# One queue instead of two for the cached pages of stick-breaking attention

## The chip, the cores and the metric

The kernel runs as one launch on one core of a Trainium2 chip. The metric is the device time of that launch in microseconds (us), lower is better. All arrays start in the device's memory (HBM) and the results go back there; the host only lays arrays out.

## The reference

One inference step of a two-layer decoder, for a prompt of 256 tokens and 8 sample sequences of 8 new tokens each. Every layer is a half-step SwiGLU, a token mixer and a second half-step SwiGLU; the weights are shared by all tokens. The first layer's mixer has two groups of heads: linear attention, and stick-breaking attention, to which the change belongs. Cut to that:

```python
def sb_mixer(q, k, v, q_base):            # per head, dh = 64, 8 heads
    z = einsum('bqhd,bkhd->bhqk', q, k) * dh ** -0.5
    before = k_pos[None, :] < q_pos[:, None]
    log_keep = where(before, log_sigmoid(-z), 0)
    after = cumsum(log_keep, axis=3, reverse=True) - log_keep
    w = where(before, exp(log_sigmoid(z) + after), 0)
    return einsum('bhqk,bkhd->bqhd', w, v)
```

For a sample sequence, k and v are 1024 cached rows followed by its 8 new ones. The cached rows lie in a pool of pages of 128 rows; a page table gives the 8 pages of each sequence. All data are 32-bit floats, so the keys of one page (128 rows by 8 heads by 64) are 256 KB, and so are its values.

## The kernel before, in words

The program is a row of stages, each a block in which every engine has its own instruction list and the lists meet only at semaphores; at the end of a block all engines wait for one another. The stages are: modulation, a feed-forward stage, the first layer's mixer (`even_stage`, from line 862), two feed-forward stages, the second layer's mixer, a last feed-forward stage. Feed-forward and projection weights stream through a ring of four 2 MB slots.

Inside the first mixer, `stick_prompt` (line 908) computes stick-breaking attention of the prompt, and `stick_sample` (line 1071) that of the 8 samples, two sequences at a time: STEPS is 4, and step g handles sequences 2g (called s = 0 in the code) and 2g + 1 (s = 1). There is one buffer of keys for each s (`K[0]`, `K[1]`, 2 MB each, eight pages) and one of values (`VV[0]`, `VV[1]`), so nothing is double-buffered across steps: the keys of step g can be loaded only when the logits of step g - 1 are done, and its values when the outputs of step g - 1 are done.

One step on TensorE (list from line 1137): wait for all 16 key pages of both sequences (line 1144) and for the queries; 32 products queries by cached keys (line 1149) and 16 by the new keys (line 1153), then `logit_ready`; wait for the weights, which ScalarE and VectorE work out (lines 1199 to 1203 and 1223 to 1232); turn them by 9 transposes (lines 1161, 1164); wait for all value pages of both sequences (line 1166); 144 products weights by values (line 1174), then `out_ready`; two transposes of the result (line 1179), which VectorE copies out (line 1248).

Loads are made by `load_pages` (line 894). For each of 8 pages it reads the page number from the table into a register with a bounds check (line 899), waits once, before the first page, for a semaphore if one is given (line 901), and issues one DMA of 256 KB (line 905). Before the change each sequence of a pair has an issuing engine of its own, by the helper `loads_of` (line 1105): SyncE (queue SP) for s = 0 and GpSimd (queue POOL) for s = 1. Each of the two does, in this order: the values of step 0 with the new rows (line 1110, 16 KB); then, for g from 1 to 3, the keys of g after `logit_ready` of g - 1, the values of g after `out_ready` of g - 1, and the new rows. The keys of step 0 are loaded in `stick_prompt`, one sequence by each of the two engines (lines 932 and 991). Within a queue the order is the program's: an instruction that waits holds up everything behind it.

GpSimd also builds small constants: six in `stick_prompt` (lines 984 to 987), four in `stick_sample` (lines 1126 to 1131), each time ahead of its loads.

The same two buffers serve all steps, and the cycle that the change concerns is these few lines:

```python
sp/pool: load_pages(K, g)   after logit_ready of g-1
sp/pool: load_pages(VV, g)  after out_ready of g-1
pe:      logits(g)          after all 16 key pages of g
pe:      values(g)          after all 16 value pages of g
```

Of the kernel before, what the change touches and what calls it, by code (L numbers as in the profile page):

```python
# [105 lines left out]
def build(nc, io):  # L106
    ctx = ExitStack()
    with ctx:
# [3 lines left out]
        def signal(name):  # L112
            return Signal(ctx, nc, name)
# [35 lines left out]
        loads = signal("loads")  # L149
# [14 lines left out]
        stored = signal("stored")  # L164
# [682 lines left out]
        logit_ready = signal("logit_ready")  # L847
# [3 lines left out]
        out_ready = signal("out_ready")  # L851
        out_read = signal("out_read")
        page_in = [signal("page_in0"), signal("page_in1")]
        value_in = [signal("value_in0"), signal("value_in1")]
        seq_ready = signal("seq_ready")
        scaled = signal("scaled")
# [51 lines left out]
        def stick_prompt(QT, KTT, V, OT, K, pages):  # L908
# [4 lines left out]
            with ExitStack() as stage:  # L913
# [7 lines left out]
                block = stage.enter_context(nc.Block(no_gpsimd_drain=True))  # L921

                @block.sync
                def _(sp):
                    store(sp, io["o_sbk"], KTT[:])
                    store(sp, io["o_sbv"][0:NPR, :].rearrange("(t p) n -> p t n", p=P), V[:, 0:2, :])
                    store(sp, io["o_sbv"][NPR:NT, :], V[0:64, 2, :])

                    sp.dma_start(io["new_rows"][0], V[0:64, 2, :]).then_inc(loads.sem, 16)
                    sp.dma_start(pages[:], io["pages"]).then_inc(loads.sem, 16)  # L930
                    sp.wait_ge(loads.sem, loads.at(32))
                    load_pages(sp, pages, 0, 0, K, io["sb_kT"], page_in[0])

                def region(kt):
                    return (0, 256, 0) if kt == 0 else (256, W, 128)
# [43 lines left out]
                @block.gpsimd  # L979
                def _(pool):  # L980

                    step = Chain(pool, pool_step)
                    step(pool.memset(mask[:], 1.0))
                    step(pool.memset(fill[:], 0.0))
                    for c0, c1, q0 in (region(0), region(1)):
                        for t, v in ((mask, 0.0), (fill, NEG)):
                            step(pool.affine_select(out=t[:, c0:c1], in_=t[:, c0:c1], compare_op=ALU.is_gt, fill=v,
                                                    base=0, pattern=[[1, c1 - c0]], channel_multiplier=-1))
                    pool_step.count = step.n
                    pool.wait_ge(loads.sem, loads.at(32))  # L990
                    load_pages(pool, pages, 0, 1, K, io["sb_kT"], value_in[0])

                @block.scalar
                def _(act):
# [76 lines left out]
        def stick_sample(QT, KTT, V, OT, K, pages):  # L1071
# [3 lines left out]
            STEPS = NB // 2  # L1075
# [3 lines left out]
            with ExitStack() as stage:  # L1079
                def tile(name, shape):  # L1080
                    return sb(name, shape, F32, stage)
                VV = [tile(f"s_V{s}", [P, NPG, 512]) for s in range(2)]
                VN = [V[0:LS, s, :] for s in range(2)]
# [15 lines left out]
                block = stage.enter_context(nc.Block(no_gpsimd_drain=True))  # L1099
# [2 lines left out]
                    (step0, rows), (step1, n) = [list(x) for x in ap.ap]  # L1102
                    return bass.AP(ap.tensor, ap.offset + step1 * (n - 1), [[step0, rows], [-step1, n]])

                def loads_of(eng, s, keys_in, values_in):

                    def new_values(g):
                        b = 2 * g + s
                        at = slice(LS * b, LS * b + LS) if isinstance(b, int) else bass.ds(b * LS, LS)
                        eng.dma_start(VN[s], io["new_rows"][0, at, :]).then_inc(values_in.sem, 16)  # L1110
                    eng.wait_ge(stored.sem, stored.at(0))
                    load_pages(eng, pages, 0, s, VV, io["sb_v"], values_in)
                    new_values(0)
                    with eng.Fori(1, STEPS) as g:
                        load_pages(eng, pages, g, s, K, io["sb_kT"], keys_in, (logit_ready.sem, logit_ready.at(0) + g))
                        load_pages(eng, pages, g, s, VV, io["sb_v"], values_in, (out_ready.sem, out_ready.at(0) + g))
                        new_values(g)

                @block.sync
                def _(sp):  # L1120
                    loads_of(sp, 0, page_in[0], page_in[1])

                @block.gpsimd
                def _(pool):
                    step = Chain(pool, pool_step)
                    step(pool.memset(QB, 0.0))

                    step(pool.memset(of_query, 0.0))
                    step(pool.affine_select(out=of_query, in_=of_query, compare_op=ALU.not_equal, fill=1.0, base=0,
                                            pattern=[[0, P // LS], [1, LS]], channel_multiplier=-1))  # L1130
                    step(pool.tensor_tensor(earlier, later[0:LS, 0:LS], ident[0:LS, 0:LS], ALU.subtract))
                    assert step.n == BUILT
                    pool_step.count = step.n

                    loads_of(pool, 1, value_in[0], value_in[1])

                @block.tensor
                def _(pe):
                    pe.wait_ge(pool_step.sem, pool_step.at(BUILT))
                    nc.tensor.matmul(PS[:, 7, 0:LS], of_query, earlier, start=True, stop=True).then_inc(summed.sem, 1)  # L1140
                    with pe.Fori(0, STEPS) as g:

                        for s in (page_in[0], value_in[0]):
                            pe.wait_ge(s.sem, s.at(LOADED) + g * LOADED)
                        pe.wait_ge(seq_ready.sem, seq_ready.at(1) + g)
                        for c in range(2):
                            for s in range(2):
                                for a in range(4):
                                    nc.tensor.matmul(PS[32 * a:32 * a + 32, c, :], QB[:, s, a, :],
                                                     K[s][:, 4 * c:4 * c + 4, a, :], start=(s == 0), stop=(s == 1))  # L1150
                        for s in range(2):
                            for a in range(4):
                                mm = nc.tensor.matmul(PS[32 * a:32 * a + 32, 2, 0:LS], QB[:, s, a, :],
                                                      KN[:, a, LS * s:LS * s + LS],
                                                      start=(s == 0), stop=(s == 1))
                        mm.then_inc(logit_ready.sem, 1)

                        pe.wait_ge(weight_ready.sem, weight_ready.at(1) + g)
                        for n in range(2):
                            for p in range(4 * n, 4 * n + 4):  # L1160
                                mm = nc.tensor.transpose(PS[:, 3 + n, (p % 4) * P:(p % 4 + 1) * P],
                                                         soft[:, 1, p * P:(p + 1) * P], ident[:])
                            mm.then_inc(turned.sem, 1)
                        nc.tensor.transpose(PS[0:LS, 5, 0:P], soft[:, 1, PAST:W], ident[:]).then_inc(turned.sem, 1)
                        for s in (page_in[1], value_in[1]):
                            pe.wait_ge(s.sem, s.at(LOADED_V) + g * LOADED_V)
                        pe.wait_ge(turned_read.sem, turned_read.at(2) + 2 * g)
                        pe.wait_ge(scaled.sem, scaled.at(2) + 2 * g)
                        for s in range(2):
                            for p in range(NPG + 1):  # L1170
                                for a in range(4):
                                    w = pT[:, p, 32 * a:32 * a + 32] if p < NPG else pT[0:LS, p, 32 * a:32 * a + 32]
                                    v = VV[s][:, p, a * P:(a + 1) * P] if p < NPG else VN[s][:, a * P:(a + 1) * P]
                                    mm = nc.tensor.matmul(PS[32 * a:32 * a + 32, 6, s * P:(s + 1) * P], w, v,
                                                          start=(p == 0), stop=(p == NPG))
                        mm.then_inc(out_ready.sem, 1)
                        pe.wait_ge(keep_ready.sem, keep_ready.at(1) + g)
                        for s in range(2):
                            mm = nc.tensor.transpose(PS[:, 7, s * P:(s + 1) * P], out_rows[:, s, :], ident[:])
                        mm.then_inc(tail_ready.sem, 1)  # L1180
# [76 lines left out]
                s.close(2 * STEPS)  # L1257
            turned.close(3 * STEPS)
            summed.close(1)
            for keys_in, values_in in (page_in, value_in):  # L1260
                keys_in.close(LOADED * STEPS)
                values_in.close(LOADED_V * STEPS)

# [1570 lines left out]
```

## Time and profile before

| what | value |
|---|---|
| runs: median (lowest to highest of 3) | 2078.24 us (2068.37 to 2079.44) |
| the profiled execution: its own time | 2079.15 us |
| the profiled execution: span, first to last instruction | 2077.6 us |
| PE busy / DVE / ACT / POOL, share of the span | 84% / 37% / 32% / 6% |
| mean granted TensorE clock | 0.89 of full speed |
| queue q1 (SP) | 317.51 MB, 40.4% of the DMA engines' span |
| queue q0 (POOL) | 33.76 MB, 5.1% |

How to read it: the span is what the trace covers; the 1.55 us between it and the execution's own time lie around it. The four steps of `stick_sample` with their set-up run from 488 us to 593.5 us after the span's start, about a twentieth of the whole. Over the whole program TensorE is the busiest engine; what bounds these four steps has to be read from their own stretch. A label SPq or POOLq is the engine's instruction list where it issues DMAs and works on registers, which the busy times leave out.

### The profile page before, as it was taken

Reading aid. Unit: us, or ns where it says so; the run is one execution under the profiler, and the core shown is the slowest. Engines: PE = TensorE matmul, PEld = TensorE weight load, DVE = VectorE, ACT = ScalarE, POOL = GpSimd, SP = SyncE. Lnnn points to the kernel's source line nnn. Section 1 sums busy time; section 2 is a strip of 40 time slices with the busy share of each in tenths; the row PEclk is TensorE's granted clock in tenths of the full one; section 3 lists DMA queues with packets and bytes.
Section 4 is the critical chain, followed back from the end, with each engine's and each line's share of the span. In section 5 each row is a group of like instructions: output and inputs, shape, how many; then the busy total and the mean of one; then the engine's idle time right before and its main releaser. Section 6 shows DMA issues by size and latency. Waiting matters only on the chain. (4 is left out here: it accounts for less than half of the span.)

```text
span 2077.6 us, 34244 instructions
## 1 busy us (share of the span) xinstructions
PE 1755.0 (84%) x13776; PEld 1510.0 (73%) x13776; DVE 776.6 (37%) x1075; ACT 671.5 (32%) x985; POOL 116.8 (6%) x241
## 2 busy tenths in 40 slices
PE   4899997965547799999799995978997677879998
PEld 3899996953335599999699993965444334579998
DVE  0534345332224333433544342410007555154443
ACT  1333324343331233332433323440016433043322
POOL 0000000012310000000000000011210122000000
PEclk8899998986756999999799995986997878989999
DMA  9666542444920466666244343342425355234430
GB/s 402 257 269 269 207 162 88 157 150 172 346 75 24 166 280 243 257 249 264 88 156 163 138 156 119 126 182 86 139 79 207 101 172 179 76 118 163 150 134 26
DMA packets 70370, 352.88 MB, mean 170 GB/s; under 512 B 11455, under 2 KB 34767, under 8 KB 54256
## 3 DMA queue, kind: packets, MB, share of 16 engines
q1 hardware_dynamic: 58992, 317.51, 40.4%
q0 software_dynamic: 11264, 33.76, 5.1%
q8 instruction: 82, 1.34, 0.3%
q14 instruction: 32, 0.26, 0.0%
HBM read 341.46 MB, written 18.03 MB: 173 GB/s over the span
## 5 line engine op out<-in xcount | busy, mean ns | idle before, releaser
L419 DVE TENSOR_TENSOR sb_Wlow<-sb_ring,sb_Whigh 128x2048 fp32r<-128x2048 f32 x136 | 311.6, 2293 | 292.0 <-ACT sb_Whigh L416 292.0
L416 ACT ACTIVATE sb_Whigh<-sb_ring 128x2048 fp32r<-128x2048 f32 x136 | 259.7, 1911 | 195.6 <-PE PS L499 195.6
L499 PE MATMUL PS<-sb_Hhigh,sb_Whigh 128*128 128x320 f32 x1408 | 244.7, 317 | 24.2 <-DVE sb_Wlow L419 12.7
L499 PEld LDWEIGHTS PS<-sb_Hhigh,sb_Whigh 128*128 128x128 f32 x1408 | 218.3, 192 | 32.0 <-issue 17.2
L499 PE MATMUL PS<-sb_Hlow,sb_Whigh 128*128 128x320 f32 x1408 | 240.9, 314 | 0.0
L499 PE MATMUL PS<-sb_Hhigh,sb_Wlow 128*128 128x320 f32 x1408 | 237.7, 311 | 0.0
L499 PEld LDWEIGHTS PS<-sb_Hlow,sb_Whigh 128*128 128x128 f32 x1408 | 217.8, 190 | 1.5
L499 PEld LDWEIGHTS PS<-sb_Hhigh,sb_Wlow 128*128 128x128 f32 x1408 | 216.5, 190 | 0.0
L590 ACT ACTIVATE sb_S<-PS 128x320 f32<-128x320 f32 x88 | 38.6, 439 | 444.9 <-PE PS L499 444.9
L633 DVE TENSOR_TENSOR sb_S<-sb_S,PS 128x320 f32<-128x320 f32 x88 | 42.9, 488 | 281.6 <-ACT sb_S L590 281.6
L499 PE MATMUL PS<-sb_Ghigh,sb_Whigh 128*128 128x320 f32 x704 | 119.2, 310 | 0.0
L499 PE MATMUL PS<-sb_Ghigh,sb_Wlow 128*128 128x320 f32 x704 | 118.9, 309 | 0.0
L499 PE MATMUL PS<-sb_Glow,sb_Whigh 128*128 128x320 f32 x704 | 118.8, 309 | 0.0
L1917 PE MATMUL PS<-sb_C,sb_w 128*128 128x512 f32 x256 | 113.7, 603 | 0.5 <-DVE sb_VC L2009 0.5
L499 PEld LDWEIGHTS PS<-sb_Ghigh,sb_Whigh 128*128 128x128 f32 x704 | 107.0, 188 | 0.8 <-issue 0.8
L499 PEld LDWEIGHTS PS<-sb_Glow,sb_Whigh 128*128 128x128 f32 x704 | 107.2, 188 | 0.0
L499 PEld LDWEIGHTS PS<-sb_Ghigh,sb_Wlow 128*128 128x128 f32 x704 | 107.2, 188 | 0.0
L271 PE MATMUL PS<-sb_ring,sb_silu_c 128*32 128x128 f32 x2304 | 79.3, 295 | 19.7 <-DMA sb_ring<-w_slots 19.7
L1917 PEld LDWEIGHTS PS<-sb_C,sb_w 128*128 128x128 f32 x256 | 48.8, 193 | 60.5 <-issue 59.6
L271 PEld LDWEIGHTS PS<-sb_ring,sb_silu_c 128*32 128x32 f32 x2304 | 67.8, 119 | 29.1 <-DMA sb_ring<-w_slots 20.9
L419 DVE TENSOR_TENSOR sb_PWlow<-sb_ring,sb_PWhigh 128x2048 fp32r<-128x2048 f32 x22 | 50.4, 2292 | 94.9 <-ACT sb_PWhigh L416 94.9
L678 PE MATMUL PS<-sb_OT,sb_ring 128*128 128x320 f32 x256 | 72.2, 446 | 9.4 <-PEq L1267 8.5
(427 smaller groups left out, 1989.5 us busy)
## 6 DMA issues: line engine op xcount, KB each, us to landing
sb_ring<-w_slots SPq DMA_DIRECT2D x119, 2048.0 KB, 7.9
sb_s_K<-sb_kT SPq DMA_DIRECT2D x32, 256.0 KB, 6.2
sb_s_K<-sb_kT POOLq DMA_DIRECT2D x32, 256.0 KB, 5.7
sb_s_V<-sb_v SPq DMA_DIRECT2D x32, 256.0 KB
sb_s_V<-sb_v POOLq DMA_DIRECT2D x32, 256.0 KB, 5.3
sb_KS<-slc_kT SPq DMA_DIRECT2D x64, 128.0 KB, 2.1
sb_C<-cmp_k POOLq DMA_DIRECT2D x32, 128.0 KB, 2.7
sb_C<-cmp_k SPq DMA_DIRECT2D x32, 128.0 KB, 2.5
```

What stands on the lines that cost most here:

```text
L271: mm = nc.tensor.matmul(PS[32 * m:32 * m + 32, 4, 0:P], silu_c32[:, k, :], ring[:, r, k, m * P:(m + 1) * P], start=(k == 0), stop=(k == KT ...
L416: nc.scalar.activation(Ws[0][:, b], columns, ACT.Copy).then_inc(high_done.sem, 1)
L419: nc.vector.tensor_tensor(Ws[1][:, b], columns, Ws[0][:, b], ALU.subtract).then_inc(low_done.sem, 1)
L499: mm = nc.tensor.matmul(to, Ws[w][:, b, q % KT, i, :], ins[x][:, q, :], start=(first and a == 0 and q == tiles[0]), stop=(last and a == 2 ...
L590: nc.scalar.activation(S[:, p % 2, :], PS[:, 2 * (p % 2), 0:NT], ACT.Silu)\
L633: nc.vector.tensor_tensor(S[:, p % 2, :], S[:, p % 2, :], PS[:, 2 * (p % 2) + 1, 0:NT], ALU.mult)\
L678: mm = nc.tensor.matmul(PS[:, 4 * half + m, 0:NT], ring[:, r, k, m * P:(m + 1) * P], OT[:, k, :], start=(k == 0), stop=(k == KT - 1))
L1917: mm = nc.tensor.matmul(PS[:, 2 * i + m, :], w1[:, i, m, a, :], C[i][:, :, :, a, :], start=(a == 0), stop=(a == 7))
```

## The change

SyncE issues all page loads of the stick-breaking stages, and GpSimd none. In `stick_prompt` SyncE loads the keys of step 0 for s = 0 and then for s = 1. In `stick_sample` it loads the values and new rows of step 0 for s = 0 and then s = 1; then in each turn of its loop the keys of both sequences (each after `logit_ready` of the step before), and then for each sequence its values (after `out_ready` of the step before) and new rows. A new pair of semaphores, `second_in`, takes the place that `value_in` had for s = 1; the second mixer still uses `value_in`. GpSimd keeps its small constants. Sizes, buffers, number of DMAs and all other engines' work stay as they were.

```diff
@@ stick_prompt, SyncE
                     load_pages(sp, pages, 0, 0, K, io["sb_kT"], page_in[0])
+                    load_pages(sp, pages, 0, 1, K, io["sb_kT"], second_in[0])
@@ stick_prompt, GpSimd
-                    pool.wait_ge(loads.sem, loads.at(32))
-                    load_pages(pool, pages, 0, 1, K, io["sb_kT"], value_in[0])
@@ stick_sample
-                def loads_of(eng, s, keys_in, values_in):
-
-                    def new_values(g):
+                @block.sync
+                def _(sp):
+                    def new_values(g, s, values_in):
                         b = 2 * g + s
                         at = slice(LS * b, LS * b + LS) if isinstance(b, int) else bass.ds(b * LS, LS)
-                        eng.dma_start(VN[s], io["new_rows"][0, at, :]).then_inc(values_in.sem, 16)
-                    eng.wait_ge(stored.sem, stored.at(0))
-                    load_pages(eng, pages, 0, s, VV, io["sb_v"], values_in)
-                    new_values(0)
-                    with eng.Fori(1, STEPS) as g:
-                        load_pages(eng, pages, g, s, K, io["sb_kT"], keys_in, (logit_ready.sem, logit_ready.at(0) + g))
-                        load_pages(eng, pages, g, s, VV, io["sb_v"], values_in, (out_ready.sem, out_ready.at(0) + g))
-                        new_values(g)
-
-                @block.sync
-                def _(sp):
-                    loads_of(sp, 0, page_in[0], page_in[1])
+                        sp.dma_start(VN[s], io["new_rows"][0, at, :]).then_inc(values_in.sem, 16)
+                    sp.wait_ge(stored.sem, stored.at(0))
+                    for s, (_, values_in) in enumerate((page_in, second_in)):
+                        load_pages(sp, pages, 0, s, VV, io["sb_v"], values_in)
+                        new_values(0, s, values_in)
+                    with sp.Fori(1, STEPS) as g:
+                        for s, (keys_in, _) in enumerate((page_in, second_in)):
+                            load_pages(sp, pages, g, s, K, io["sb_kT"], keys_in, (logit_ready.sem, logit_ready.at(0) + g))
+                        for s, (_, values_in) in enumerate((page_in, second_in)):
+                            load_pages(sp, pages, g, s, VV, io["sb_v"], values_in, (out_ready.sem, out_ready.at(0) + g))
+                            new_values(g, s, values_in)
@@ stick_sample, GpSimd
-                    loads_of(pool, 1, value_in[0], value_in[1])
@@ stick_sample, TensorE
-                        for s in (page_in[0], value_in[0]):
+                        for s in (page_in[0], second_in[0]):
...
-                        for s in (page_in[1], value_in[1]):
+                        for s in (page_in[1], second_in[1]):
```

## Rows read from the trace of the kernel before

**Rows 1.** Two steps: length, busy PE, PEld, DVE, ACT, POOL, clock, DMA share, GB/s.

```profile
517.90:542.10 24.20, 11.76 (x203) 7.60 (x203) 6.73 (x10) 8.72 (x13) 9.17 (x17) 0.79 0.96 349
...
567.00:593.50 26.50, 13.66 (x203) 8.13 (x203) 6.68 (x9) 7.66 (x8) 3.99 (x8) 0.68 0.43 152
```

**Rows 2.** Timeline of TensorE, 488 to 594 us; start, duration, instruction.

```profile
490.80 6.34 PE L1149 MATMUL PS<-sb_s_K,sb_H 128*32 128x512 f32 x32 [0.80 <-ACT sb_H L1194]
...
511.04 3.06 PE L1174 MATMUL PS<-sb_s_V,sb_OT 128*32 128x128 f32 x64 [0.57 <-DVE sb_OT L1235]
...
517.91 3.64 PE L1149 MATMUL PS<-sb_s_K,sb_H 128*32 128x512 f32 x32 [0.24 <-issue]
...
542.12 3.64 PE L1149 MATMUL PS<-sb_s_K,sb_H 128*32 128x512 f32 x32 [0.30 <-DMA sb_s_K<-sb_kT]
...
567.00 5.34 PE L1149 MATMUL PS<-sb_s_K,sb_H 128*32 128x512 f32 x32 [1.13 <-DMA sb_s_K<-sb_kT]
572.15 0.29 PE L1153 MATMUL PS<-sb_OT,sb_H 128*32 128x8 f32 x16
...
586.23 3.01 PE L1174 MATMUL PS<-sb_s_V,sb_OT 128*32 128x128 f32 x64 [0.57 <-DVE sb_OT L1235]
```

**Rows 3.** Timeline of VectorE, the last instruction of the stage.

```profile
592.98 0.47 DVE L1248 COPY sb_OT<-PS 64x64 f32 x2 [0.66 <-PE PS L1179]
```

**Rows 4.** Timeline of SyncE's queue, 488 to 536 us; start of first, time to end of last.

```profile
488.68 7.96 SPq L905 DMA_DIRECT2D sb_s_V<-sb_v  x8
496.68 0.38 SPq L1110 DMA_DIRECT2D sb_V<-new_rows  x1
498.25 8.95 SPq L905 DMA_DIRECT2D sb_s_K<-sb_kT  x8
516.88 7.95 SPq L905 DMA_DIRECT2D sb_s_V<-sb_v  x8
525.02 0.34 SPq L1110 DMA_DIRECT2D sb_V<-new_rows  x1
526.90 8.73 SPq L905 DMA_DIRECT2D sb_s_K<-sb_kT  x8
```

**Rows 5.** Line 899, the page number's read; duration min/median/max in ns, first and last start.

```profile
L899 SPq FUSED_REGOPS  x85: 51/152/178, 446.4 to 572.3; - x85
...
L899 SPq TENSOR_LOAD <-sb_s_pages x64: 263/268/482, 445.9 to 572.0; - x64
```

**Rows 6.** Line 905, the page's DMA, from both engines, and its time to landing.

```profile
L905 SPq DMA_DIRECT2D sb_s_K<-sb_kT x32: 332/333/393, 447.3 to 559.3; - x32
L905 POOL DMA_DIRECT2D sb_s_K<-sb_kT x32: 537/539/697, 447.5 to 560.3; - x32
...
DMA to landing us min/median/max: 2.8/5.7/8.5
```

**Rows 7.** SyncE's queue in the second mixer: pages of 128 KB, half the size.

```profile
1475.38 8.69 SPq L1835 DMA_DIRECT2D sb_C<-cmp_k  x8
```

**Rows 8.** What SyncE's queue waited for, 488 to 594 us; total, times, longest.

```profile
SPq L905 <- PE PS L1174: 18.3, 3, 9.0
```

**Rows 9.** DMA queue q1, 515 to 541 us; packets, MB, share of 16 engines' time.

```profile
q1 hardware_dynamic: 2313, 4.20, 45.2%
```

**Rows 10.** The same for the first 40 us of the program, one queue.

```profile
q1 hardware_dynamic: 1544, 15.73, 94.6%
```

**Rows 11.** Line 1110, the new rows' DMA: its time to landing.

```profile
DMA to landing us min/median/max: 5.5/5.6/6.0
```

**Rows 12.** Windows on TensorE: length, busy, granted clock, DMA share, GB/s.

```profile
490.80:497.20 6.40, 6.40 (x48) 0.57 0.86 279
517.90:521.60 3.70, 3.69 (x48) 1.00 0.86 270
532.68:534.90 2.22, 2.18 (x9) 0.50 1.04 388
567.00:572.40 5.40, 5.40 (x48) 0.68 0.98 327
```

More of the change, by code:

```diff
@@ L853, in build @@
         page_in = [signal("page_in0"), signal("page_in1")]
+        second_in = [signal("second_in0"), signal("second_in1")]
         value_in = [signal("value_in0"), signal("value_in1")]
@@ L1259, in stick_sample @@
             summed.close(1)
-            for keys_in, values_in in (page_in, value_in):
+            for keys_in, values_in in (page_in, second_in):
                 keys_in.close(LOADED * STEPS)
```

## The prediction

> **What bounds the stage now.** I read the windows of the steps first, then TensorE's timeline, then SyncE's queue. The windows show a full step: 24.20 us with TensorE busy for half of it and the DMA engines for 0.96 of it, at 349 GB/s; the last step, which prefetches no keys, is at 0.43 [rows 1]. The timeline tells whether those transfers are late. Logits start at 490.80, 517.91, 542.12 and 567.00 us, and the idle time that a key page ended before them is 0.30 and 1.13 us in steps 2 and 3, none in steps 0 and 1 [rows 2]. So a step is as long as its chain logits, weights, transposes, values, and the two queues deliver the next keys just in time. The slack is thin: the reader should see that pages arrive with about 1 us missing, not with 10 us to spare.
>
> SyncE's queue shows what a page costs its issuer. Eight value pages take 7.95 us from the first issue to the end of the last, so with the last DMA's own 0.33 us their spacing is (7.95 - 0.33)/7 = 1.09 us; eight key pages in the loop take 8.73 to 8.95 us, spacing 1.20 us [rows 4, 6]. This is the instruction list's time, not the transfer's: the table read takes 0.27 us, a register operation 0.15 us and the DMA instruction 0.33 us, with next to no spread [rows 5, 6], and pages of half the size are issued no faster, eight in 8.69 us [rows 7]. Key pages have extra register operations, 51 ns the shortest (85 operations for 64 pages: the 21 surplus ones match 7 pages in 3 turns) [rows 5]. SyncE is already most of the way to full: in three steps it waited 18.3 us in all for outputs [rows 8], some 6 us of each 24.
>
> **What the change does, part by part.** *GpSimd's issues go* (64 pages and 4 rows). Its 0.54 us each [rows 6] ran beside everything else; TensorE is never held by GpSimd's issuing except through landed pages, so the removal gains 0 by itself. *The prompt stage* gives SyncE 16 key pages instead of 8 from 447.3 on [rows 6]; at 1.09 us each they are issued by 465 and needed at 490.80 [rows 2], so 25 us cover them: 0. *The new semaphores* replace others one for one: 0.
>
> *Step 0's values.* SyncE issues the first sequence's from 488.68 and its new rows at 496.68 [rows 4]; the second sequence's pages start 1.1 us later, 497.8, and its new rows go out 8.0 us after that, at 505.8. A page lands 2.8 us after issue at best, 5.7 us in the median [rows 6], new rows after 5.6 us [rows 11]. The values are multiplied at 511.04 [rows 2]: between 2 us early and 0.4 us late. I take 0, and no lateness there matters, since keys come later still.
>
> *The loop is where it costs.* One turn on SyncE now holds 32 pages and two sets of new rows:
> - keys: 15 spacings of 1.20 = 18.0 us from the first issue to the last;
> - on to the first value page: 1.1 us;
> - values: 7 spacings of 1.09 = 7.6, new rows 0.5 later, 1.1 to the next page, 7.6 and 0.5 again = 17.4 us (from 516.88, 525.02) [rows 4];
> - back to the next turn's first key: 526.90 - 525.02 = 1.9 us [rows 4].
>
> That is 38.4 us a turn, against a chain of 24.2. Twice SyncE's old work without its waits says the same: 2 by (24.2 - 6.1) = 36.2, and two joints of 1.1 us that a wait hid before.
>
> The turns then follow. First key of step 1: 505.8 plus 1.57 (496.68 to 498.25) [rows 4] = 507.4. Last key page of step 1 at 507.4 + 18.0 = 525.4, of step 2 at 563.8, of step 3 at 602.2. Both waits in the queue have long passed by then: keys of a step are allowed once the logits of the one before are done, values once the outputs are. By my times (logits, then the same 19 us of chain from their end) outputs 0, 1 and 2 are done near 517, 554 and 592, and SyncE reaches the values of steps 1, 2 and 3 at 526.5, 564.9 and 603.3. So SyncE never waits again. Were it to wait for outputs, the second sequence's values and the next step's 16 key pages would stand behind that wait; before, only one sequence's did.
>
> *Landing.* The bounds are 2.8 us (the shortest) and 5.7 us (the median, with both queues in flight and the engines 0.96 busy) [rows 1, 6]. Now 256 KB leave every 1.09 or 1.20 us, about 0.6 of the old rate, so I take a page on emptied engines, 2.9 us. Logits of step 3 start at 605.1 instead of 567.00: **+38.1 us**.
>
> *The clock.* After an idle stretch of 11 us (521.6 to 532.68) [rows 2, 12] the transposes ran at a granted 0.50, the lower of the two levels, 1.2 GHz; the logits took 6.40 us at 0.57, 5.40 at 0.68 and 3.70 at 1.00 [rows 12]. In the changed kernel TensorE idles more than 10 us before each set of logits. In steps 1 and 2 this is hidden behind SyncE; in step 3 the logits take 6.4 where they took 5.4: **+1.0** (bounds 0 and 1.0; 0 if the clock climbs as in step 3 of before).
>
> *The tail* from those logits to the last copy (572.44 to 593.45) [rows 2, 3] is the same chain. It needs step 3's values 13.8 us after the logits (586.23 - 572.44), at 605.1 + 6.4 + 13.8 = 625.3; SyncE issues the last of them, the new rows, at 603.3 + 17.4 = 620.7, and they land between 623.5 and 626.3: 0 taken, 1.0 at worst.
>
> Sum: +39.1 us on the profiled execution's 2079.15 us (span 2077.6), which is 2118.3. That execution is 0.9 us above the median of the runs, so I forecast **2117 us**. Unknown either way: value pages may need the keys' register operations (16 by 0.11 by 3 = +5 us) or the keys lose theirs (-5); landing up to +2.8; values +1; clock -1. Added up, about -6 and +9. The runs before lay 10 us below to 1 us above their median.
>
> **The rivals.**
> *The queue as bound.* Half the traffic took the SP queue 45.2% of the engines' time [rows 9]; all of it on one queue might not drain as fast. In the 24.2 us step one queue moved 4.2 MB, 174 GB/s; were that its ceiling, 8.4 MB would need 48 us a turn, 10 more than SyncE, and the time would be 2117 + 30 = 2147. Against it: in the first 40 us the same queue alone moved 15.73 MB at 94.6% [rows 10], 394 GB/s, though in larger packets. It decides if the ceiling is under 8.4 MB / 38.4 us = 219 GB/s. Chance 0.05.
>
> *The issue is hidden, and nothing changes.* For this, SyncE's spacing would have to fall to 24.2 us / 32, about 0.7 us a page, as it could if part of the 1.09 us were waiting for GpSimd's traffic. The evidence against is the constant 333 ns, and the half-size pages at the same spacing [rows 6, 7]. The time would stay at 2078. The Trainium skill, "DMA: Bandwidth & Descriptors", section "Issuing engines are not separate DMA queues", says that issuing from several engines saves only the sequencer's time to initiate, which is usually small beside the DMA. By that rule the sum would be 0; this trace agrees that both queues share the 16 engines, but shows an issue spacing of 1.09 us beside a page's 0.7 us at 349 GB/s, so here that part is not small. Chance 0.05.
>
> *Keys first pays, not slower.* If SyncE keeps up and both sequences' keys go ahead of any values, the key waits (1.13 + 0.30 us) go, and TensorE stays at its upper clock into step 3 (5.34 to 3.64): 3.1 us less, 2075. It decides where a page's spacing is below 0.7 us, as above. Chance 0.03.
>
> *The change does not do what it says*: SyncE's list already holds the first sequence; only the second's issue moves. If GpSimd had been the late one of the two, some delay would be taken out. GpSimd's last key DMA in the trace starts 1 us after SyncE's (560.3 and 559.3) [rows 6], so this is worth 1 us: 2077. Chance 0.02.
>
> **How the numbers follow.** Forecast 0.85, the queue 0.05, hidden issue 0.05, keys first 0.03, the last 0.02. Half a per cent, 10.4 us, is what can be told from no change. The first two are slower: 0.90. The other three are within it, less 0.02 for a faster run: same 0.08, faster 0.02. The range takes the unknowns, and below them the runs' scatter: 2117 - 6 - 8 = 2103 to 2117 + 9 + 1 = 2127.
>
> **What would show it.** SyncE's queue without a gap over 2 us from 488 to 621 us; 16 key pages in about 18 us; TensorE waiting 10 to 14 us for a key page before each of the logits of steps 1 to 3; starts near 528, 566 and 605; DMA share near 0.6 in these turns; everything after the stage shifted by 39 us. It is wrong if SyncE's spacing shrinks below 0.9 us without GpSimd, if landing grows from page to page (the queue), or if TensorE waits for values rather than keys.

## The result and the profile after

| | before | after |
|---|---|---|
| median (lowest to highest) | 2078.84 us (2068.37 to 2079.63, 4 runs) | 2117.84 us (2116.91 to 2121.45, 4 runs) |
| profiled execution: own time, span | 2079.15, 2077.6 us | 2116.91, 2115.3 us |
| granted TensorE clock, mean | 0.890 | 0.881 |

The ratio is 1.0199, with a 95% interval of 1.0168 to 1.0230: the change costs some 39 us, 1.7 to 2.3%, and the forecast was 2117 us.

The two spans differ by 37.7 us. Nearly all of it lies between SyncE's first value page and the last copy of the stage. That was 593.45 - 488.68 = 104.8 us [rows 3, 4] and is now 629.67 - 486.79 = 142.9 us: +38.1. The rest lies outside the stage and was not traced further: the stage begins 1.9 us earlier in this execution, and what follows it is 1.5 us longer. The stage's last copy in the changed kernel, the counterpart of [rows 3]:

```profile
629.20 0.47 DVE L1245 COPY sb_OT<-PS 64x64 f32 x2 [0.66 <-PE PS L1176]
```

SyncE's queue in the changed kernel, in order of time (start of the first, time to the end of the last), the counterpart of [rows 4]:

```profile
486.79 8.35 SPq L906 DMA_DIRECT2D sb_s_V<-sb_v  x8
495.18 0.38 SPq L1110 DMA_DIRECT2D sb_V<-new_rows  x1
496.52 7.97 SPq L906 DMA_DIRECT2D sb_s_V<-sb_v  x8
504.53 0.38 SPq L1110 DMA_DIRECT2D sb_V<-new_rows  x1
506.11 18.28 SPq L906 DMA_DIRECT2D sb_s_K<-sb_kT  x16
525.15 7.96 SPq L906 DMA_DIRECT2D sb_s_V<-sb_v  x8
533.29 0.35 SPq L1110 DMA_DIRECT2D sb_V<-new_rows  x1
534.61 8.37 SPq L906 DMA_DIRECT2D sb_s_V<-sb_v  x8
543.17 0.34 SPq L1110 DMA_DIRECT2D sb_V<-new_rows  x1
545.06 18.05 SPq L906 DMA_DIRECT2D sb_s_K<-sb_kT  x16
...
583.45 18.04 SPq L906 DMA_DIRECT2D sb_s_K<-sb_kT  x16
```

The list has no gap over 1.6 us any more. Sixteen key pages take 18 us, and a turn of the loop 545.06 - 506.11 = 39.0 us, then 583.45 - 545.06 = 38.4. In the loop the view of SyncE's waits shows none for logits or outputs; before, it held 18.3 us of waiting for outputs [rows 8].

TensorE's timeline, the logits of the four steps and, of step 3, the products by the new keys and the first values (in brackets: idle before, and what ended it), the counterpart of [rows 2]:

```profile
488.89 6.32 PE L1146 MATMUL PS<-sb_s_K,sb_H 128*32 128x512 f32 x32 [0.79 <-ACT sb_H L1191]
...
527.24 5.91 PE L1146 MATMUL PS<-sb_s_K,sb_H 128*32 128x512 f32 x32 [11.52 <-DMA sb_s_K<-sb_kT]
...
565.79 5.42 PE L1146 MATMUL PS<-sb_s_K,sb_H 128*32 128x512 f32 x32 [12.31 <-DMA sb_s_K<-sb_kT]
...
604.14 5.02 PE L1146 MATMUL PS<-sb_s_K,sb_H 128*32 128x512 f32 x32 [12.87 <-DMA sb_s_K<-sb_kT]
608.99 0.28 PE L1150 MATMUL PS<-sb_OT,sb_H 128*32 128x8 f32 x16
...
623.05 2.41 PE L1171 MATMUL PS<-sb_s_V,sb_OT 128*32 128x128 f32 x64 [0.57 <-DVE sb_OT L1232]
```

Here the reader should see where the 39 us sit: three waits for key pages of 11.5 to 12.9 us, 36.7 in all, where there were 0.3 and 1.1. No value product waits for a page. The rest of the 38.1 is in the logits of steps 1 and 2, which run slower, 4.1 us in all with the new keys' products; step 3 gives 0.9 us back.

Line 906 (905 before), the page's DMA and its landing, the counterpart of [rows 6]; below it the DMA queue from 506 to 545 us (packets, MB, share of 16 engines' time), that of [rows 9]:

```profile
L906 SPq DMA_DIRECT2D sb_s_K<-sb_kT x64: 332/333/392, 445.6 to 601.2; - x64
...
DMA to landing us min/median/max: 2.6/2.9/3.5
```

```profile
q1 hardware_dynamic: 4742, 8.61, 75.5%
```

Pages land faster than before, 2.9 us in the median for 5.7. The transfers are not late; they are issued late.

### The profile page after: what moved, and what is told of

It reads as the page before. It is cut to its first block and busy times, and to the rows that moved or that the text cites. A ratio compares the mean times of both kernels' runs of the same rounds, so it can differ in the third digit from the quotient of the medians.

```text
span 2115.3 us, 34234 instructions
## 1 busy us (share of the span) xinstructions
PE 1759.7 (83%) x13776; PEld 1511.1 (71%) x13776; DVE 776.2 (37%) x1075; ACT 670.1 (32%) x985; POOL 79.7 (4%) x173
```

## The experiments

Each ratio is to runs of the kernel before that were taken beside it on the same chip: median 2077.37 us (7 runs) for the first four, 2079.41 us (17 runs) for the last two. The edits are cut to the lines that matter; `...` marks what is left out.

**Half the bytes.** In the changed kernel, every loop page is cut to half its columns:

```diff
-                eng.dma_start(dst, src[bass.ds(page, 1), :, :].rearrange("a p n -> p (a n)"))\
+                cols = slice(0, 512 if isinstance(at, int) else 256)
+                eng.dma_start(dst[:, cols], src[bass.ds(page, 1), :, cols].rearrange("a p n -> p (a n)"))\
```

> The changed kernel, but in SyncE's loop each page DMA moves only the first half of the columns (128 KB instead of 256 KB; steps 1 to 3 work on half-old pages, so this part of the computation is left out). Same number of DMAs, same register work. Theory (the issuing list is the bound): nothing moves, page spacing stays 1.09 us (values) and 1.18 us (keys), a turn of the loop stays near 38.5 us, logits start near 527, 565 and 603 us, time 2117 us, within 4 us. Rival (the transfers on one queue are the bound): half the bytes take half the time, the turn falls to the chain of 24 us and the time to about 2080 us.

Measured: 2117.95 us, ratio 1.0201 (1.0184 to 1.0219), the same as the changed kernel. SyncE's queue and the landing in this run:

```profile
505.65 18.58 SPq L907 DMA_DIRECT2D sb_s_K<-sb_kT  x16
524.99 7.95 SPq L907 DMA_DIRECT2D sb_s_V<-sb_v  x8
...
544.88 18.07 SPq L907 DMA_DIRECT2D sb_s_K<-sb_kT  x16
```

```profile
DMA to landing us min/median/max: 2.0/2.1/3.1
```

A turn is 544.88 - 505.65 = 39.2 us with 109 GB/s on the queue as it was 39.0 with 222. Only the landing got shorter, by 0.8 us. The bytes are not the bound.

**Page numbers kept.** The same DMAs, but a step's values use the page numbers that its keys read:

```diff
...
-                page = eng.value_load(cell, min_val=0, max_val=NPOOL - 1)
+                if numbers is None or len(numbers) < NPG:
+                    page = eng.value_load(cell, min_val=0, max_val=NPOOL - 1)
+                    if numbers is not None:
+                        numbers.append(page)
+                else:
+                    page = numbers[p]
...
```

> The changed kernel, but the page numbers that SyncE reads for the keys of a step are kept in registers and used again for its values, so that in the loop half of the table reads and checks go; DMAs, queue, order and bytes stay. Theory (the list is the bound, and 0.7 us of each page's 1.09 us is the number's read): value pages go out every 0.40 to 0.45 us, a turn falls from 38.5 to about 28 us, the waits before the logits of steps 1 to 3 go from 11.5, 12.3, 12.9 us to about 11.5, 2 and 2, and the time to 2096 us (2092 to 2101). Rival (the cost sits in the DMA instruction or in the queue's draining): spacing of values stays at 1 us or their landing grows by as much, turn 38 us, time 2117 us.

Measured: 2097.63 us, ratio 1.0109 (1.0090 to 1.0128). SyncE's queue, and TensorE's logits of steps 1 to 3:

```profile
505.74 18.56 SPq L911 DMA_DIRECT2D sb_s_K<-sb_kT  x16
524.40 3.73 SPq L911 DMA_DIRECT2D sb_s_V<-sb_v  x8
528.31 0.34 SPq L1115 DMA_DIRECT2D sb_V<-new_rows  x1
528.74 3.94 SPq L911 DMA_DIRECT2D sb_s_V<-sb_v  x8
532.86 0.31 SPq L1115 DMA_DIRECT2D sb_V<-new_rows  x1
534.70 18.02 SPq L911 DMA_DIRECT2D sb_s_K<-sb_kT  x16
```

```profile
527.33 5.42 PE L1152 MATMUL PS<-sb_s_K,sb_H 128*32 128x512 f32 x32 [12.43 <-DMA sb_s_K<-sb_kT]
...
556.10 6.39 PE L1152 MATMUL PS<-sb_s_K,sb_H 128*32 128x512 f32 x32 [3.28 <-DMA sb_s_K<-sb_kT]
...
583.91 3.64 PE L1152 MATMUL PS<-sb_s_K,sb_H 128*32 128x512 f32 x32 [0.86 <-DMA sb_s_K<-sb_kT]
```

Eight value pages take 3.7 us instead of 8, a turn 29.0 us, and half of the loss is gone, though all 32 pages still go through one queue. So more than half of the price, 0.60 of 1.09 us, is the read of the page number with its register operations and its check, which are gone where the number is kept. The spacing, (3.73 - 0.33)/7 = 0.49 us, is a little above the 0.40 to 0.45 expected: in this burst the DMA instruction itself took 0.38 us in the median instead of 0.33.

The same burst settles the rival of a slow queue. From 524 to 536 us one queue carried everything:

```profile
GB/s 225 266 335 137 82 239 348 178 362 376 341 335 307 376 328 260 225 259 321 403 369 362 410 389 396 410 410 376 382 410 396 417 403 389 389 410 369 396 382 389
...
q1 hardware_dynamic: 2236, 4.07, 97.6%
```

In the second half of this stretch it moved 362 to 417 GB/s (each figure is for a fortieth of the 12 us), no less than the 349 GB/s of both queues together over a step before [rows 1].

**Half of the change.** The second sequence's values and new rows go back to GpSimd, both sequences' keys stay on SyncE:

```diff
...
                     with sp.Fori(1, STEPS) as g:
                         for s, (keys_in, _) in enumerate((page_in, second_in)):
                             load_pages(sp, pages, g, s, K, io["sb_kT"], keys_in, (logit_ready.sem, logit_ready.at(0) + g))
-                        for s, (_, values_in) in enumerate((page_in, second_in)):
-                            load_pages(sp, pages, g, s, VV, io["sb_v"], values_in, (out_ready.sem, out_ready.at(0) + g))
-                            new_values(g, s, values_in)
+                        load_pages(sp, pages, g, 0, VV, io["sb_v"], page_in[1], (out_ready.sem, out_ready.at(0) + g))
+                        new_values(sp, g, 0, page_in[1])
...
+                    with pool.Fori(1, STEPS) as g:
+                        load_pages(pool, pages, g, 1, VV, io["sb_v"], second_in[1], (out_ready.sem, out_ready.at(0) + g))
+                        new_values(pool, g, 1, second_in[1])
```

> Half of the change: SyncE issues the keys of both sequences and the first sequence's values; the second sequence's values and new rows go back to GpSimd. Theory (32 pages on one list are too many): SyncE's turn is 18.0 + 1.1 + 7.6 + 0.5 + 1.9 = 29.1 us against the chain of 24.2; from a first key page at 498.3 the last key page of step 3 goes out at 574.5 and lands near 578, 11 us later than before: 2090 us (2086 to 2095). Rival (it is a matter of the keys' order or of a single queue, not of the count): either all of the 39 us or none, 2117 or 2078 us.

Measured: 2090.84 us, ratio 1.0066 (1.0049 to 1.0083). SyncE's queue:

```profile
498.10 18.25 SPq L906 DMA_DIRECT2D sb_s_K<-sb_kT  x16
...
527.14 18.01 SPq L906 DMA_DIRECT2D sb_s_K<-sb_kT  x16
...
556.38 18.03 SPq L906 DMA_DIRECT2D sb_s_K<-sb_kT  x16
```

TensorE's waits for keys (total, times, longest):

```profile
PE PS L1151 <- DMA sb_s_K<-sb_kT: 13.0, 3, 8.2
```

A turn is 29.0 and 29.2 us. The loss goes with the number of pages on SyncE's list: with 16 a turn (the kernel before) TensorE waits 1.4 us in all for keys [rows 2], with 24 it waits 13.0 us and the run is 13.5 us longer, with 32 it waits 36.7 us and the run is 39 us longer.

**Order by sequence.** The same 32 pages on SyncE, each sequence's keys and values together:

```diff
-                        for s, (keys_in, _) in enumerate((page_in, second_in)):
+                        for s, (keys_in, values_in) in enumerate((page_in, second_in)):
                             load_pages(sp, pages, g, s, K, io["sb_kT"], keys_in, (logit_ready.sem, logit_ready.at(0) + g))
-                        for s, (_, values_in) in enumerate((page_in, second_in)):
                             load_pages(sp, pages, g, s, VV, io["sb_v"], values_in, (out_ready.sem, out_ready.at(0) + g))
                             new_values(g, s, values_in)
```

> The changed kernel with one thing altered: in SyncE's loop the order is keys, values, new rows of the first sequence, then keys, values, new rows of the second, instead of both sequences' keys first. Same count on the same list. Theory (the list is in order, so the second sequence's keys now stand behind the first one's wait for outputs): the loop turns into output, 8 value pages, 8 key pages, landing, logits, chain, output, about 45 us a turn; SyncE waits again, some 8 us or more before the first sequence's values; logits of step 1 start 9 us later than in the changed kernel, those of step 3 about 24 us later, time 2141 us (2134 to 2148). Rival (only the count of issues matters, the order does not): 2117 us.

Measured: 2144.19 us, ratio 1.0331 (1.0313 to 1.0348), 26 us worse than the changed kernel. What SyncE's queue waited for, and TensorE for the keys (total, times, longest):

```profile
SPq L906 <- PE PS L1170: 15.2, 2, 8.5
```

```profile
PE PS L1145 <- DMA sb_s_K<-sb_kT: 61.1, 3, 21.0
```

The second sequence's keys now stand behind the first one's wait for outputs, and TensorE waits 61.1 us for keys instead of 36.7. Of these two orders keys first is the better on a single list, by 26 us, so in the changed kernel the order makes up for part of what one list costs. One detail was off: SyncE waits in two of the turns, not in three, since in step 1 it reaches the values only at 517.4 us, by which time the outputs that it would wait for are done.

**All on GpSimd.** The changed kernel's loads, in the same order, on the other engine; the edit is against the kernel before:

```diff
...
-                @block.sync
-                def _(sp):
...
+                    with pool.Fori(1, STEPS) as g:
+                        for s, (keys_in, _) in enumerate((first_in, second_in)):
+                            load_pages(pool, pages, g, s, K, io["sb_kT"], keys_in, (logit_ready.sem, logit_ready.at(0) + g))
...
```

> The changed kernel with all page loads of the stick-breaking stages on GpSimd's queue instead of SyncE's; same order, same count. Theory (a single list in order is the bound, whichever engine holds it): page spacing 1.22 us (keys) and 1.14 us (values) as in GpSimd's half before, a turn of 18.3 + 1.2 + 17.9 + 1.8 = 39 to 40 us, first values 2 us later behind the constants; logits of step 3 start 6 to 9 us later than in the changed kernel, 2125 us (2121 to 2130). Rival (the cost is particular to SyncE's way of issuing): spacing on GpSimd falls below 0.8 us once it is alone, and the time is near 2080 us.

Measured: 2127.27 us, ratio 1.0236 (1.0215 to 1.0256). GpSimd's timeline, the first of key pages, the ninth, and the first of the next turn:

```profile
510.06 0.56 POOL L907 DMA_DIRECT2D sb_s_K<-sb_kT  x1 [0.86 <-issue]
...
519.85 0.54 POOL L907 DMA_DIRECT2D sb_s_K<-sb_kT  x1 [0.72 <-issue]
...
550.12 0.56 POOL L907 DMA_DIRECT2D sb_s_K<-sb_kT  x1 [1.21 <-issue]
```

Eight key pages take 9.79 us, 1.22 each, and a turn 40.1 us. It is the single list, not SyncE. GpSimd's list costs 48 us against 39 by the medians (the two intervals overlap a little). Part of the difference is a wait that the expectation did not have: twice TensorE waits for new rows before the values.

```profile
PE PS L1171 <- DMA sb_V<-new_rows: 4.9, 2, 2.8
```

**A try at beating both.** The kernel before, with both queues, each keeping its page numbers (the edit of the second experiment, except that the first page's number is read again):

```diff
...
+                        kept = []
-                        load_pages(eng, pages, g, s, K, io["sb_kT"], keys_in, (logit_ready.sem, logit_ready.at(0) + g))
-                        load_pages(eng, pages, g, s, VV, io["sb_v"], values_in, (out_ready.sem, out_ready.at(0) + g))
+                        load_pages(eng, pages, g, s, K, io["sb_kT"], keys_in, (logit_ready.sem, logit_ready.at(0) + g), kept)
+                        load_pages(eng, pages, g, s, VV, io["sb_v"], values_in, (out_ready.sem, out_ready.at(0) + g), kept)
```

> The kernel before (both queues), but each queue keeps the page numbers read for a step's keys and uses them for its values, save the first. Theory (before, the chain of the steps is the bound and the keys came about 1 us late): the values of a step leave in 3.5 us instead of 8 on SyncE, the next keys start some 4 us earlier, the key waits of 0.3 and 1.1 us go and the logits of step 3 run at the upper clock: 3 us less, about 2075 us, hardly to be told from no change. Rival (the DMA engines, 0.96 busy in a step, are the bound): keys and values land no earlier, 2078 us or a little more.

Measured: 2078.88 us, the median of 12 runs, ratio 1.0002 (0.9988 to 1.0015). In the stage the theory holds; SyncE's first value page, the logits of steps 1 to 3 and the last copy:

```profile
488.09 7.97 SPq L910 DMA_DIRECT2D sb_s_V<-sb_v  x8
...
517.12 3.64 PE L1155 MATMUL PS<-sb_s_K,sb_H 128*32 128x512 f32 x32 [0.26 <-issue]
...
541.21 3.64 PE L1155 MATMUL PS<-sb_s_K,sb_H 128*32 128x512 f32 x32 [0.23 <-issue]
...
565.21 3.64 PE L1155 MATMUL PS<-sb_s_K,sb_H 128*32 128x512 f32 x32 [0.23 <-issue]
...
589.09 0.47 DVE L1254 COPY sb_OT<-PS 64x64 f32 x2 [0.66 <-PE PS L1185]
```

These logits wait for no page and run at a granted 1.00, the upper level, and a step is 24.0 to 24.1 us; the stage, from SyncE's first value page at 488.09 to the end of the last copy at 589.56, takes 101.5 us instead of 104.8. Those 3.3 us cannot be seen in the whole: the 17 runs of the kernel before lie between 2067.82 and 2084.23 us. Some 0.5 us are also lost outside the span: 2.0 to 2.1 us lie there in every run of this kernel, where 1.6 to 1.7 lay before; what makes the difference was not tried. So it beats the changed kernel but not, measurably, the one before.

## Why the prediction was right

**The price of a page** was the step that carried it, and it held: (7.96 - 0.33)/7 = 1.09 us for a value page, 17.7 us from the first of 16 key pages to the last (601.2 - 583.45) for a forecast 18.0, a turn forecast at 38.4 and measured at 39.0 and 38.4. Neither of the 5 us held open for register operations came. That it is the list's own time was argued from half-size pages in another stage; the half-bytes run shows it in this one, and the kept page numbers show that 0.60 us of it go with the number's read. One reading was off: the extra register operations are not the key pages' own. In the run with half of the change, GpSimd's loop holds value pages alone, and these go out every (524.71 - 516.15)/7 = 1.22 us, where before, behind the keys, they went out every 1.13; the extra comes with whichever pages of a sequence a turn loads first.

**The cascade** held: no wait is left on SyncE, TensorE waits for keys and never for values, and the logits of step 3 start 604.14 - 486.79 = 117.4 us after SyncE's first page where they started 567.00 - 488.68 = 78.3 [rows 2, 4]: +39.0, forecast +38.1. Of the missing 0.9 us, 0.6 is the way to the first key page of step 1: 506.11 - 486.79 = 19.3 us, forecast 507.4 - 488.68 = 18.7. Another 0.6 is in the first turn, the second was as forecast, and the key pages of step 3 took 0.3 us less.

**Landing** held: I took a page on emptied engines, 2.9 us; the median is 2.9.

**The clock's term** failed in sign. I added 1.0 us on the ground that after an idle stretch of 10 us and more the logits of step 3 would run as those of step 0, at 0.57 in 6.4 us [rows 12]. They and the values behind them ran faster than before. TensorE's windows of the changed kernel, the logits of steps 0 to 3 (length, busy, granted clock, DMA share, GB/s):

```profile
488.89:495.30 6.41, 6.41 (x48) 0.58 0.74 218
...
527.24:533.20 5.96, 5.96 (x48) 0.61 0.82 239
...
565.79:571.30 5.51, 5.51 (x48) 0.67 0.86 253
...
604.14:609.20 5.06, 5.05 (x48) 0.72 0.82 234
```

The granted clock of the logits rises from step to step, although the idle stretch ahead of them grows from 11.5 to 12.9 us. Read in stretches of half a microsecond, each of the four sets begins at 0.50, the lower level, and ends at 1.00; in step 0 the rise comes between 5.0 and 5.5 us after the start of the logits, in step 3 between 2.5 and 3.0. With 5.13 us to the end of the new keys' products instead of 5.44, and first values in 2.41 us instead of 3.01 [rows 2], step 3 gave back 0.9 us where I charged 1.0. The two misses, 0.9 in the cascade and 1.9 here, have opposite signs, so the stage came out at +38.1 against a forecast of +39.1. That this is as close as 1 us is partly luck, and so is a median within 1 us of 2117, where the four runs of the kernel before spread over 11.

**The rivals.** The slow queue is refuted by the burst at 362 to 417 GB/s. The hidden issue is refuted: spacing did not shrink with GpSimd issuing no pages. The Trainium skill, "DMA: Bandwidth & Descriptors", section "Issuing engines are not separate DMA queues", states that DMAs issued by different engines run on the same 16 DMA engines. These traces agree: one queue reached the rate of two. The Trainium skill adds in the same section that the time to initiate a DMA is usually small beside the DMA itself. That did not hold here, for 256 KB pages whose numbers are read at run time: 1.09 us of issuing stand beside 0.63 to 0.72 us of transfer at the burst's rates (at the 349 GB/s that the prediction used it is 0.75 us, not 0.7). Keys first gains 26 us against the other order on a single list; with two lists no other order was tried.

Another reading was off without touching the sum: I expected a DMA share near 0.6 in these turns, by the rate, and it was 0.755.

## What to carry to other kernels

Before merging two issuing lists, count what one turn puts on the list: DMAs times their spacing in the timeline (not their transfer time), plus loop overhead, and compare it with the turn's length; here 16 pages fitted into 24 us, and 24 and 32 did not. If the DMA's address is read at run time, the read and its checks can cost more than the DMA instruction; keeping the numbers in registers for a second use took a value page from 1.09 to 0.49 us here. On a single list whose instructions go out in order, put what is needed first ahead of anything that waits for a later event.

## What the runs showed that was not expected

The DMA engines' busy share is not proportional to what they move. In the changed kernel one queue at 222 GB/s shows 75.5%, where 222 of the burst's some 390 GB/s would be 57%. The half-bytes run (506 to 545 us) and all on GpSimd (510 to 549 us) show:

```profile
q1 hardware_dynamic: 4653, 4.24, 36.2%
...
q0 software_dynamic: 2587, 8.32, 72.2%
```

That is 36.2% at 109 GB/s and 72.2% at 214. These three are in proportion to one another; the burst, 97.6% at 339 GB/s on average, is not. As the same queue reached 362 to 417 GB/s in the burst, a share of 0.75 should not be read as three quarters of the capacity.

The mean clock of the logits after 11 to 13 us without any matrix work was anything from 0.61 to 0.72 in this one execution, while transposes after 11 us without, in 2.2 us, ran at 0.50 throughout in the kernel before [rows 12]. What sets the moment of the rise was not tried further; a term of 1 us could not be placed from such rows.
